# MLP of a two-layer encoder step: sample rows held stationary, token sums formed and stored by GpSimd

## What is computed

```python
D_MODEL = 1024; SEQ = 1024; DEC_BATCH = 8; DEC_SEQ = 16; D_FF = 4 * D_MODEL
h = rmsnorm(x, norm_mlp[i])
x = x + jnp.square(jax.nn.relu(h @ mlp_w_up[i])) @ mlp_w_down[i]
```

## Time and profile before

| | us |
|---|---|
| median of three runs | 3002.1 (2995.62 to 3002.98) |
| profiled execution | 3004.56 |
| its span | 3002.5 |
| mean granted clock of PE | 0.967 |
| PE busy, share of the span | 93% |
| MLP of the first layer, up part | about 632 to 1029 |
| MLP of the first layer, down part | about 1029 to 1443 |
| MLP of the second layer, up part | about 2165 to 2562 |
| MLP of the second layer, down part | about 2562 to 2974 |

### The profile page before, as it was taken

The page is one execution under the profiler, slowest core; times in us unless marked ns, Lnnn a source line. Parts: engine busy times, 40 slices in busy tenths (PEclk is TensorE's granted clock), DMA queues, the critical chain, the costliest instruction groups (busy, mean ns, idle before and its releaser), DMA issues. The chain is left out here.

```text
span 3002.5 us, 41024 instructions
## 1 busy us (share of the span) xinstructions
PE 2792.1 (93%) x15235; PEld 2344.3 (78%) x15235; DVE 1814.2 (60%) x2158; ACT 1130.5 (38%) x2127; POOL 1016.9 (34%) x666
## 2 busy tenths in 40 slices
PE   7989997999999899998799999998999999899995
PEld 6878886788888777776698877776888888677774
DVE  5656662374444588889510028885654444888886
ACT  4344444233222233332322239995332222332332
POOL 3100002042222265565221216662322221665554
PEclk9999998999999999998899999999999999999997
DMA  4311114322222632220235356745122223522201
GB/s 138 87 54 44 42 51 153 133 69 90 90 93 90 216 109 91 88 92 15 76 123 163 126 146 164 171 122 176 57 93 90 90 90 116 214 88 92 88 32 70
DMA packets 227733, 310.12 MB, mean 103 GB/s; under 512 B 21088, under 2 KB 143456, under 8 KB 227552
## 3 DMA queue, kind: packets, MB, share of 16 engines
q1 hardware_dynamic: 227552, 307.68, 32.4%
HBM read 212.83 MB, written 94.80 MB: 102 GB/s over the span
## 5 line engine op out<-in xcount | busy, mean ns | idle before, releaser
L1878 POOL TENSOR_TENSOR m_uprS<-m_upr 128x512 f32<-128x512 f32 x64 | 84.5, 1321 | 525.0 <-DMA m_upr<-in_mlp_w_up 525.0
L1683 ACT COPY m_part<-m_ps 128x512 f32<-128x512 f32 x96 | 56.3, 586 | 268.3 <-PE m_ps L76 268.3
L2041 DVE TENSOR_TENSOR m_z<-m_ps,m_part 128x512 f32<-128x512 f32 x96 | 66.2, 690 | 145.1 <-PE m_ps L76 126.5
L2186 DVE TENSOR_TENSOR x<-m_ps,x 128x1024 f32<-128x1024 f32 x128 | 150.3, 1211 | 4.5 <-PE m_ps L76 4.5
L1897 POOL TENSOR_TENSOR m_wop1l<-m_wr,m_wop1h 128x1024 fp32r<-128x1024 f32 x32 | 87.6, 2737 | 134.3 <-ACT m_wop1h L1740 134.3
L2029 DVE TENSOR_TENSOR m_upS2l<-m_uprS,m_upS2h 128x512 fp32r<-128x512 f32 x32 | 38.0, 1186 | 126.4 <-ACT m_upS2h L1676 126.1
L1096 POOL TENSOR_TENSOR c_wo0l<-c_wo0r,c_wo0h 128x1024 fp32r<-128x1024 f32 x1 | 2.3, 2348 | 330.6 <-ACT c_wo0h L1076 330.6
L74 PE MATMUL m_ps<-m_wop0h,m_uop0h 128*128 128x512 f32 x128 | 60.9, 476 | 48.2 <-DVE x L2186 43.9
L1740 ACT CAST m_wop1h<-m_wr 128x1024 fp32r<-128x1024 f32 x32 | 33.7, 1052 | 184.2 <-DVE m_wr L2162 102.9
L2108 DVE TENSOR_TENSOR m_ur<-m_ur,m_ur 128x1024 f32<-128x1024 f32 x48 | 101.9, 2122 | 0.2
L3102 ACT ACTIVATE e_b<-e_ps 128x512 f32<-128x512 f32 (+3 forms) x192 | 95.8, 499 | 12.4 <-PE e_ps L3298 11.8
(11 more groups left out here) (929 smaller groups left out, 10269.0 us busy)
## 6 DMA issues: line engine op xcount, KB each, us to landing
m_upr<-in_mlp_w_up SPq DMA_DIRECT2D x32, 1024.0 KB, 6.0
scratch_u<-m_u SPq DMA_DIRECT2D x128, 256.0 KB, 2.0
m_wr<-in_mlp_w_down SPq DMA_DIRECT2D x64, 512.0 KB, 6.8
m_ur<-scratch_u SPq DMA_DIRECT2D x64, 512.0 KB, 5.6
scratch_x<-x SPq DMA_DIRECT2D x18, 512.0 KB, 2.6
x<-scratch_x SPq DMA_DIRECT2D x4, 2048.0 KB, 10.5
scratch_qr<-a_qrst SPq DMA_DIRECT2D x9, 512.0 KB, 3.4
a_x<-in_x_prompt SPq DMA_DIRECT2D x8, 512.0 KB, 4.9
```

What stands on the lines that cost most here:

```text
L1683: act.copy(part[i][:], src).then_inc(parted.sem, 1)
L1878: pool.tensor_tensor(up_sum[n][:], up_source(ins[0], p), up_source(ins[1], p), ALU.add if n == "S1" else ALU.subtract).then_inc(up_summed. ...
L2041: dve.tensor_tensor(z[out][:], src, part[kept_part][:], ALU.add).then_inc(joined.sem, 1)
L2186: dve.tensor_tensor(out, src, out, ALU.add).then_inc(summed.sem, 1)
```

## The change

**Up part.** `up_sample` now holds the sample rows: they are PE's stationary operand, and two blocks of 128 columns of weights (A11 and A21, then A12 and A22) are moved past them in one matmul of 256 columns. For that the blocks of a pair of tiles, `up_1` and `up_2`, lie in one tile each; in `up_1` the two lie 22 KB apart. The result is tokens x features, so after DVE has squared it, PE turns it with two transposes (`flip_sample`, after P2 of the next pair) and ACT copies it out of PSUM (`copy_sample`). After each pair POOL forms S1 to S4 of the tokens from the stored results (`u_sums`), ahead of the weight sums, which it now forms two pairs ahead; SP stores seven arrays (A11, A22, A12, S1 to S4) in place of four.

**Down part.** SP loads seven token arrays a chunk through a ring of six places, one after the other as they come free; DVE forms no token sums any more. The tokens' operands rotate over four slots in the order of use. T1 and T2 are formed by POOL (`weight_sum`), in the order given by `first_weights`. T1 and T3 have places of their own. DVE adds after each product its two halves and then makes the low part of the operand four products ahead (`accumulate_both`). The sample steps add up in their PSUM banks over all chunks, and DVE adds them to x only in the last. The first loads of the down part and the last stores of the up part are ordered anew on SP.

The core of the diff:

```diff
-TOKEN_OPERANDS = ("A11", "A12", "A22", "S1", "S2", "S3", "S4")
-WEIGHT_OPERANDS = ("B11", "B12", "B21", "B22", "T1", "T2", "T3", "T4")
+TOKEN_OPERANDS = ("A11", "S2", "S3", "S1", "A12", "S4", "A22")
+WEIGHT_OPERANDS = ("B11", "T2", "T3", "T1", "B21", "B22", "B12", "T4")
...
+        def token_raw(c, n):
+
+            m = 7 * c + TOKEN_OPERANDS.index(n)
+            return tok_raw[m % 6], tok_in[m % 6].sem, 16 * (m // 6 + 1)
+
+        def token_slot(c, n):
+            return tok_slots[(7 * c + TOKEN_OPERANDS.index(n)) % 4][0]
...
             def store_u(p, i):
 
-                j, cols = ((0, slice(0, 512)), (1, slice(512, 1024)), (1, slice(0, 512)), (0, slice(512, 1024)))[i]
-                sp.wait_ge(u_done.sem, 5 * p + (1, 2, 4, 5)[i])
-                sp.dma_start(scratch["u"][2 * p + j, :, cols], u_st[i][:]).then_inc(u_out[i].sem, 16)
+                sp.wait_ge(u_done.sem, 5 * p + (1, 2, 4)[i])
+                sp.dma_start(scratch["u"][i, p],
+                             u_st[i][:]).then_inc(u_out[i].sem, 16)
+
+            def store_u_sums(p):
+                for i, n in enumerate(("S1", "S2", "S3", "S4")):
+                    sp.wait_ge(u_summed.sem, u_sum_at(p, n))
+                    sp.dma_start(scratch["u"][3 + i, p], u_st[3 + i][:]).then_inc(u_out[3 + i].sem, 16)
 
...
+            for p in range(LAST):
+                if p + 2 < PAIRS_FF:
+                    sp.wait_ge(up_lo.sem, up_at("A22", p))
+                    sp.wait_ge(up_summed.sem, 4 * (p + 1))
+                    load_up(p + 2)
+                if p:
+                    store_u_sums(p - 1)
+                store_u(p, 0)
+                store_u(p, 1)
+                if p:
+                    store_sample_u(p - 1)
+                store_u(p, 2)
...
+            sp.wait_ge(prod.sem, up_done(LAST, "P3"))
+            load_tokens(0, "S1")
+            store_u_sums(LAST)
+            store_sample_u(LAST)
+            load_tokens(0, "A12")
+            load_tokens(0, "S4")
...
+            for c in range(1, CHUNKS):
+                if c >= 2:
+                    sp.wait_ge(down.sem, down_at(c - 2, "s1"))
+                    for n in WEIGHT_OPERANDS:
+                        sp.wait_ge(wt_lo[n].sem, c - 1)
                 load_sample_tokens(c)
-                for n in WEIGHT_OPERANDS:
-                    sp.wait_ge(wt_lo[n].sem, c - 1)
                 for q in ("11", "12", "21", "22"):
                     load_weights(c, q)
+                for i, n in enumerate(TOKEN_OPERANDS):
+                    before, j = divmod(7 * c + i - 6, 7)
+                    sp.wait_ge(tok_lo[TOKEN_OPERANDS[j]].sem, before + 1)
+                    load_tokens(c, n)
...
+            def copy_sample(p):
+
+                act.wait_ge(us_flipped.sem, p + 1)
+                after(act, us_out[p % 2], 16 * (p // 2))
+                act.copy(us_st[p % 2][:], up_banks(p)[3][:, 2 * P:4 * P].rearrange("p (j c) -> p j c", j=2)).then_inc(
+                    us_copied.sem, 1)
...
-                act.copy(out[:], token_source(c, n)[:]).then_inc(tok_hi[n].sem, 1)
+                    raw, arrived, count = token_raw(c, n)
+                    act.wait_ge(arrived, count)
+                    out = token_slot(c, n)[0]
+                    before, j = divmod(7 * c + TOKEN_OPERANDS.index(n) - 4, 7)
+                    if before >= 0:
+                        act.wait_ge(down.sem, down_at(before, DOWN_ORDER[j]))
+                    elif n != "A11":
+                        act.wait_ge(prod.sem, up_done(PAIRS_FF - 1, "P5" if n == "S2" else "P4"))
+                act.copy(out[:], raw[:]).then_inc(tok_hi[n].sem, 1)
...
             weight_hi(0, "T2")
+            copy_sample(PAIRS_FF - 1)
+            token_hi(0, "S3")
+            weight_hi(0, "T3")
+            token_hi(0, "S1")
+            weight_hi(0, "T1")
             token_hi(0, "u8")
-            weight_hi(0, "T1")
-            weight_hi(0, "T3")
...
-                token_hi(c, "S3")
                 token_hi(c, "A12")
                 weight_hi(c, "B21")
...
                 if more:
-                    token_hi(c + 1, "S1")
                     token_hi(c + 1, "A11")
                     weight_hi(c + 1, "B11")
                     token_hi(c + 1, "S2")
                     weight_hi(c + 1, "T2")
+                    token_hi(c + 1, "S3")
+                    weight_hi(c + 1, "T3")
+                    token_hi(c + 1, "S1")
                     weight_hi(c + 1, "T1")
                     token_hi(c + 1, "u8")
-                    weight_hi(c + 1, "T3")
...
+            up_sums(1, ("S1", "S2", "S3", "S4"))
+
+            def u_sums(p):
+
+                for n, out, a, b, op in (("S1", 3, 3, 1, ALU.add), ("S2", 4, 3, 0, ALU.subtract),
+                                         ("S3", 5, 1, 4, ALU.subtract), ("S4", 6, 2, 4, ALU.subtract)):
+                    if n == "S1":
+                        pool.wait_ge(u_done.sem, 5 * p + 5)
+                    else:
+                        pool.wait_ge(u_summed.sem, u_sum_at(p, "S1" if n == "S2" else "S2"))
+                        after(pool, u_out[out], 16 * p)
+                    pool.tensor_tensor(u_st[out][:], u_st[a][:], u_st[b][:], op).then_inc(u_summed.sem, 1)
+
+            for p in range(PAIRS_FF):
+                u_sums(p)
+                if p + 2 < PAIRS_FF:
+                    up_sums(p + 2, ("S1", "S2", "S3", "S4"))
 
...
+            def weight_sum(c, n):
...
-                pool.wait_ge(*weight_in(c, "22"))
-                if c:
-                    pool.wait_ge(down.sem, down_at(c - 1, "s1"))
+                out, a, b = {"T1": (sum_t1, raw["12"], raw["11"]), "T2": (raw["11"], raw["22"], sum_t1),
+                             "T3": (sum_t3, raw["22"], raw["12"]), "T4": (raw["11"], raw["21"], raw["11"])}[n]
+                if n == "T1":
+                    pool.wait_ge(*weight_in(c, "11"))
+                    pool.wait_ge(*weight_in(c, "22"))
+                    after(pool, wt_lo["T1"], c)
+                elif n == "T2":
+                    pool.wait_ge(wt_summed.sem, weight_sum_at(c, "T1"))
+                    pool.wait_ge(wt_lo["B11"].sem, c + 1)
+                elif n == "T3":
+                    after(pool, wt_lo["T3"], c)
+                    if c == 0:
+                        pool.wait_ge(prod.sem, up_done(PAIRS_FF - 1, "P3"))
                 else:
-                    pool.wait_ge(prod.sem, 9 * PAIRS_FF)
...
+            def first_weights(c):
+                weight_lo(c, "B11")
+                weight_sum(c, "T1")
+                weight_sum(c, "T2")
+                weight_lo(c, "T2")
+                weight_sum(c, "T3")
+                weight_lo(c, "T3")
+                weight_lo(c, "T1")
+
+            first_weights(0)
             pool.wait_ge(x_back[0].sem, 16)
             pool.wait_ge(x_back[1].sem, 16)
             pool.tensor_tensor(x[:, 0:4, 512:1024], x[:, 0:4, 512:1024], x[:, 4:8, 512:1024],
...
 
             token_lo(0, "S2")
-            weight_sums(0)
+            token_lo(0, "S3")
             token_lo(0, "S1")
             token_lo(0, "u8")
             for c in range(CHUNKS):
                 last = c == CHUNKS - 1
-                token_sum(c, "S3")
-                token_lo(c, "S3")
-                for hp in range(2):
-                    accumulate(c, "P1", hp)
-                token_lo(c, "A12")
-                for hp in range(2):
-                    accumulate(c, "P6", hp)
-                token_sum(c, "S4")
-                token_lo(c, "S4")
+
+                def accumulate_both(n, ahead=4):
+
+                    for hp in range(2):
+                        accumulate(c, n, hp)
+                    later, j = divmod(7 * c + DOWN_ORDER.index(n) + ahead, 7)
+                    if later < CHUNKS:
+                        token_lo(later, TOKEN_OPERANDS[j])
+
+                accumulate_both("P1")
+                accumulate_both("P6")
                 if last:
-                    join_totals("P6", "P1", [(summed, down_at(c, "P6"))])
-                for hp in range(2):
-                    accumulate(c, "P7", hp)
-                token_lo(c, "A22")
+                    join_totals("P6", "P1", [(summed, summed_at(c, "P6"))])
+                accumulate_both("P7")
                 if last:
                     join_totals("P3", "P6", [(join_2, 2)])
-                    join_totals("P7", "P6", [(summed, down_at(c, "P7"))])
-                for hp in range(2):
-                    accumulate(c, "P5", hp)
+                    join_totals("P7", "P6", [(summed, summed_at(c, "P7"))])
+                accumulate_both("P5")
                 if last:
-                    join_totals("P3", "P5", [(summed, down_at(c, "P5")), (join_2, 4)])
+                    join_totals("P3", "P5", [(summed, summed_at(c, "P5")), (join_2, 4)])
                     join_totals("P4", "P7", [(join_2, 6)])
+                accumulate_both("P2")
+                if last:
+                    accumulate_sample(0)
```

(47 more changed lines are left out.)

305 lines of the change are left out of this document (110 added, 195 removed).

## The result

The changed kernel takes 2948.0 us (median of 4 runs, 2946.0 to 2953.4) against 3002.5 us for the kernel before (4 runs): ratio 0.9824, 95% interval 0.9803 to 0.9846. The forecast was 2937 with a range of 2900 to 2970. The profiled execution took 2948.7 us (span 2946.0), 55.9 less than the profiled one of before (3004.6).

A forecast was written before the change was run, and what follows sets the result against it. PE's own instructions bound the up part; in the down part PE also waits for DVE's additions. 3004.6 - 70.4 (up) + 20.8 (turn) - 1 (chunks) - 14.5 (last chunk) = 2939.5, 2937 beside the median; range 2900 to 2970 us.

The forecast's parts named there:

- Up part: Up part's sample step: 24 matmuls 0.12 us apart replace 48, plus two transposes; 2.2 us a pair, 70 us gained.
- lower estimate: Up part by the skill page's pitches, 81 ns and 109 ns: 1.0 us a pair, 32 us gained in all.
- sign of being wrong: Up part: PE idling there because POOL's sums come late would show the forecast wrong.
- Steady chunks: Down part: stall moves from P1 to P6, 3.45 us idle; chunk 48.6 us against 48.7; gain 1 us for twelve chunks.
- Turn: Up to down: P1 waits for POOL's B11 low part, P7 starts at 35.9 instead of 25.5; loss 21 us in all.
- Last chunk: From P1 to P4's start: 51.4 us against 60.2 and 57.3 before, gain 14.5 us.
- price of the clock: After PE stalls over some 3 us, slower clock adds 1.6 to 2.6 us; 3.3 in the last chunk.
- (1): Down part's queue chain a turn or two shorter: idle under 2.5 us, no clock loss, 2905 us; chance 0.20.
- (2): Down part's queue chain one or two turns longer, 1.15 us each in 14 chunks: 2953 to 2969 us; chance 0.12.
- (3): Up part's wide matmuls, two blocks apart, 0.17 us apart: 32 us gained in all, 2975 us; chance 0.06.
- (5): Up part's wide matmuls run at 0.227 us and flips cost 10 us: within 0.3% or slower, 3015; chance 0.03.
- (4): POOL becomes the down part's gate, slower than before: at 55 us a cycle, 3027 us; chance 0.04.

The follow-up runs named there:

- e1_narrow: Changed kernel with the up part's sample step issued as 48 matmuls of 128 columns instead of 24 of 256, sample rows still stationary: 3027.9 us.
- e2_dup: Changed kernel with POOL's sum T3 computed twice in the chunks after the first: 2982.6 us.
- e3: Changed kernel; after the first chunk ACT makes u8's and S1's high parts before T3's, DVE u8's low part before P4's additions: 2902.0 us.
- e11: Changed kernel, two queues reordered: ACT makes S3's high part before T2's, S1's before T3's, u8's last; DVE u8's low part behind P1's additions: 2875.3 us.
- e6: Changed kernel with the down part's weight sums T1 and T2 made by DVE again instead of POOL: 2874.4 us.
- e4_turn: Changed kernel, turn reordered: POOL makes B11 low to T3's sum before the last token sums; ACT copies the sample before T2 high, S1, u8 before T3: 2937.1 us.
- e8_best: e6 plus e4_turn (first chunk's T1 and T2 left on POOL), e7, and u8's low part behind P1's additions: 2858.9 us.
- e10_more: e8_best with A12 and S4 loaded before the last stores, first chunk's A12 and u8 low parts behind P6's copies, last chunk's P5 additions before joins: 2850.2 us.
- e7: Changed kernel with each pair of DVE's joins in the last chunk one product later: 2941.1 us.

## Why the prediction was right, and where it was not

**Up part: right to 0.1 us in 70, the last 2 us of it by luck.** The pitch of 0.12 taken from the attention's 256 columns held although the moving operand is two blocks 22 KB apart, and e1_narrow shows the width to be the cause. In e1_narrow, as in the kernel before, 48 matmuls of 128 columns take 5.31 us, 0.111 apart. The lower estimate (32 us), from the Trainium skill's page "TensorE: Matmul & The Clock Gate", section "Back-to-back issue gap", had them 0.081 apart; it is refuted. The row decided rightly. A pair gained 2.27 us, not 2.2, which would make 72.6 us. The first pair of each layer gave some 1.2 of that back in its wait for T4's low part, a term that the forecast did not have. Its sign of being wrong, idle time in the up part, so appeared once a layer, but through DVE and not through POOL's sums. These and the flips cost PE nothing but the flips' own 0.23 us.

**Steady chunks: right, by the named mechanism.** From P3's start at 1194.32, forecast and measured: POOL's T1 begins at 3.7 (1198.04, 3.7), T3's sum is done at 16.5 (1210.8, 16.5), P1's first half is added at 25.15 (half of the pair of 2.34 us from 1218.17, 25.0); idle 3.45 (3.19). The forecast's chunk of 48.6 us came in eight of twelve; in four it was 49.7 to 49.9, for the clock (see the last section), hence a mean of 49.0. DVE's idle time showed ahead of S1's low part (2.06 us) and not of u8's. e2_dup showed that POOL's part of the chain carries through one to one, e3, e11 and e6 that taking it off DVE's additions frees them. What the forecast did not draw from its own chain is that three moves in the order of ACT's and DVE's queues were worth another 73 us.

**Turn: right.** P1 10.2 us after the last P3, as forecast to the digit; P7 at 35.5 and 34.4 (35.9). e4_turn adds what the forecast left out: behind POOL's queue stands the next gate, P6's copy behind A12's load, so removing the 10 us before P1 gives back only 3 to 5 of them a layer in the first chunk.

**Last chunk: the mis-sized term.** -14.5 forecast (its own parts, 8.8 and 5.9, add up to 14.7), -5.4 measured. Forecast: idle times of 3.45, 4.75, 0.85 and 0.9, and 3.3 for the clock. PE's timeline of layer 1 (the other layer has 3.19, 4.10, none over 0.1, and 2.79):

```profile
1366.40 0.80 PE L74 MATMUL m_ps<-m_wop1h,m_uop2h 128*128 128x512 f32 x1 [3.21 <-DVE m_Z L2190]
1383.35 0.80 PE L74 MATMUL m_ps<-m_wop3h,m_uop0h 128*128 128x512 f32 x1 [4.36 <-DVE m_Z L2190]
1391.29 0.50 PE L74 MATMUL m_ps<-m_wop1h,m_uop1h 128*128 128x512 f32 x1 [0.75 <-DVE x L2190]
1402.56 0.50 PE L74 MATMUL m_ps<-m_wop2h,m_uop2h 128*128 128x512 f32 x1 [2.82 <-DVE x L2190]
```

In this layer three of the four idle times are as forecast within 0.4 us. The fourth, before P3's second half, is 2.8 instead of 0.9 in both layers: DVE's joins there, four operations, take 9 us together, one turn behind POOL's low part of T4 and one behind POOL's own joins,

```profile
1392.40 4.51 DVE L2205 TENSOR_TENSOR x<-x 128x1024 f32<-128x1024 f32 x2
1396.83 4.54 DVE L2205 TENSOR_TENSOR x<-x,m_Z 128x1024 f32<-128x1024 f32 x2
1401.29 2.34 DVE L2190 TENSOR_TENSOR x<-m_ps,x 128x1024 f32<-128x1024 f32 x2
```

and P2's addition stands behind them. The larger part is the clock: with 38.1 us of work and 11.1 and 10.1 of idle time, 5.7 and 9.0 us are left for it, not 3.3. So the step that failed is the price of the clock: I had given four stalls 3.3 us in total; each stall of some 3 us has its own price, and it is not a constant (below).

**The rivals.** (1), a chain a turn shorter, did not come about of itself. (2), a chain one or two turns longer, is what e2_dup made of it: +36 us for 2.35 us more on the chain, where 14 chunks of 2.35 are 33. (3) and (5) are excluded by the pitch of 0.12. (4) did not come about, and e11_queue shows that POOL's load is not the gate: with POOL doing T1 and T2 (e11_queue, 2875.3) the kernel is as fast as e6_dve with DVE doing them (2874.4), and a steady chunk is 0.3 us longer than in e8_best. So the Trainium skill's rule in "GPSIMD Engine Reference", section "Engine selection", to keep such sums off POOL, does not decide this case, though its factor of about two holds here too (2.35 against 1.21).

What stays open: how much of the first chunk's remaining 17 us (60.8 against 43.6) POOL's sums of the last pair hold. The trace of e10_more has 11.1 us of idle time there: 3.00 before P6 for T2's low part, 4.60 before P7 for T3's, which stands behind those four sums in POOL's queue (6.09 us), and 3.49 before P5's second half for P7's copy. Open is also whether a join order exists that delays neither P3's addition nor the norm. Neither was tried.

## What to carry to other kernels

When an engine idles for a bank, follow the releasing operation back through the queues and ask of each predecessor whether the late one needs it; here an addition out of PSUM waited for two low parts, over a cast, for a weight sum it has nothing to do with, and moving entries within two queues was worth more than the whole change (73 us against 55). Put what frees the bottleneck's buffers ahead of what only must be ready later, and after each such swap look for the operation that it delayed: three of the edits here (e3, e4, e7) brought up a new stall that took back a third or more of the gain that I expected. Price each stall over some 2 us by itself, with the clock behind it and as a range over all the stalls of that length in the trace, rather than all of them in one sum.
